# A transformer block pair on one core: token operands of the down projection split in order of use, a third buffer for the high parts of its weights, and its sixth and seventh products exchanged

## The chip, the cores and the metric

The kernel runs on one NeuronCore of a Trainium2 chip. The metric is the device time of one execution in microseconds. The kernel before takes 1577.86 us (median of 3 runs, 1577.79 to 1578.15).

## The reference

Two transformer blocks run one after the other over 512 tokens of width 1024: first a mixer with a mixture of experts, then a mixer, a cross attention and a gated feed-forward layer. The change touches only the last matrix product, the down projection of that feed-forward layer (hidden width 2816 = 22 x 128):

```python
h = rms_norm(x, norm_ffn[l])
x = x + (jax.nn.silu(h @ w_gate[l]) * (h @ w_up[l])) @ w_down[l]
```

All matrices are float32. The kernel keeps that precision by cutting each operand into a high part (rounded to the fast matmul type) and a low part (the rest), and adding three matmuls: high x high, low x high, high x low.

## The kernel before

**The products.** With A the hidden activations (A11, A12 for tokens 0 to 255, A21, A22 for tokens 256 to 511, by halves of the hidden width) and B the weights (B11, B12 / B21, B22, by halves of hidden width and of output columns), the 2 x 2 block product is done with seven products instead of eight (Winograd's form of Strassen's method). In the order of the kernel before they are P1 = A11 B11, P2 = A12 B21, then P6, P7, P4 together, then P3, then P5. Each product has 11 *chunks* (128 rows of the hidden width, 512 output columns). A chunk needs 6 matmuls of 128x512: two token tiles, three matmuls each (`product`). P6, P7 and P4 need sums of the four weight blocks. For these, 11 *triples* T0 to T10 are loaded into one slot each (three rows of 256 KB), a fourth row is added onto one of them by an accumulating DMA of 256 KB from POOL (`add_weights`), and DVE then makes two further sums in place (`weight_sums`, two TENSOR_TENSOR of 128x512; their events are called T2 and T4 in the code, which is not a number of a triple). A triple feeds 18 matmuls. P5 needs the sum of two transferred blocks: each of its three slots is loaded by SP and then gets a second block of 1 MB (the last 768 KB) added onto it by a DMA from POOL (`sums_last`). P3 needs a plain block.

**The slots.** SP issues all loads in order; each waits until PE has freed the slot. Slots 1, 2, 0 serve P1 and again P2; the triples take slots 9, 10, 1, 2, 0, 9, 10, 1, 2, 0, 9; then P3 takes 10, 1, 2 and P5 takes 0, 9, 10, the last of these the slot of P3's first four chunks. So the slot of a triple is that of the triple five before it.

**The splitting.** Chunks are split in *units*: u0 to u5 are P1, u6 to u11 P2 (two chunks each, the sixth one chunk), u12 to u22 the triples T0 to T10, u23 to u34 the last two products. ACT rounds a unit into a cell of the buffer CHH (`unit_high`) and DVE subtracts to make the low part in the slot (`unit_low`); PE waits for the low part. The token operands are split in four pieces each (three chunks, the last two): ACT writes the high piece into a buffer HA (`high_of`), DVE the low piece into AO (`low_of`). A triple uses the pieces of S2, S3 and A22 that hold its chunk. P3 uses S4, P5 uses S1.

**What sets the order.** Each of ACT, DVE and POOL is one queue that runs strictly in the order of the code. The loop over `units` in `scalar` and `vector` is written by hand: at each u it says which pieces, sums and additions onto the output rows (`add_on`) stand there. In `vector` the weight sums of a triple stand ahead of the low part of the unit at which they are called:

```python
if 11 <= u < 11 + FK:
    weight_sums(u - 11)
if u >= len(EARLY_UNITS):
    unit_low(*unit)
```

so the low part of triple j (unit 12 + j) stands behind the sums of triple j + 1.

Of the kernel before, what the change touches and what calls it, by code (L numbers as in the profile page):

```python
# [9 lines left out]
F32R = mybir.dt.float32r  # L10
# [3 lines left out]
ALU = mybir.AluOpType  # L14
# [10 lines left out]
FT = 22  # L25
FK = 11
# [31 lines left out]
GAINED = 33, 38, 46, 52  # L58
FFN_TURN = 11, 15, 27, 33
EARLY_UNITS = 8, 10, 12  # L60


class Issued:
# [6 lines left out]
class Counts:  # L70
# [17 lines left out]
    def at(self, event):  # L88
        if event is None or self.known is None:
            return None, 0  # L90
        name, value = self.known[event]
        return self.sem(name), value
# [278 lines left out]
def _build(nc, t, ctx, force_dense):  # L371
# [8 lines left out]
    at, mark, newest = counts.at, counts.mark, counts.newest  # L380
# [3 lines left out]
    def place(name, kb, n, dt=F32):  # L384
        return nc.alloc_sbuf_tensor_at(name, [P, n * KB], dt, offset=base + kb * 1024)

    CHH = place("CHH", 24, 16, F32R)
    R1, R2 = place("R1", 40, 16), place("R2", 56, 16)
    AH, AL = place("AH", 72, 16, F32R), place("AL", 88, 16, F32R)
    YH, YL = place("YH", 104, 8, F32R), place("YL", 112, 8, F32R)  # L390
# [4 lines left out]
    XTF = place("XTF", 88, 16, F32R)  # L395
    ATF = place("ATF", 168, 8, F32R)
    AR, AO = place("AR", 104, 77), place("AO", 104, 77, F32R)
    HA = [place(f"HA{n}", kb, 11, F32R) for n, kb in enumerate((181, 40, 72, 83, 126))]
    CHX = place("CHX", 52, 4, F32R)
    small_at = [194 * 1024]  # L400

    def sb(name, cols, dt=F32):
# [78 lines left out]
    def plan_slot(i, src, nk, n, part):  # L481
        s = Slot()
        s.number, s.nk, s.n, s.part = len(slots), nk, n, part
        s.src, s.rest, s.more = src, None, None
        s.ap, s.low = (x[i][:, 0:nk * n].rearrange("p (k n) -> p k n", k=nk) for x in (slot_mem, slot_low))
        taken[i] += 1
        s.i, s.landed, s.former, held[i] = i, 16 * taken[i], held[i], s
        slots.append(s)
        return s
# [25 lines left out]
    in_turn = itertools.cycle((2, 0, 1))  # L515
# [23 lines left out]
    in_turn = itertools.cycle((1, 2, 0))  # L539
# [18 lines left out]
    D0 = len(CH)  # L558
    units, hi_of = [], {}

    def unit(s, q0, n, at, ready):
        u = len(units)
        of = CHX if at == 8 else CHH
        a = (0 if at == 8 else at) * 512
        chunks = range(len(CH), len(CH) + n)
        for i, c in enumerate(chunks):
            CH.append((s, q0 + i))
            hi_of[c] = of[:, a + i * 512:a + (i + 1) * 512]
        cells = range(at, at + n)
        before = [holds_cell[x] for x in cells if x in holds_cell]  # L570
        holds_cell.update((x, chunks[-1]) for x in cells)
        units.append((chunks, s.ap[:, q0:q0 + n, :], s.low[:, q0:q0 + n, :],
                      of[:, a:a + n * 512].rearrange("p (k n) -> p k n", k=n), before, ready))
# [1 line left out]
    holds_cell = {(D0 - 1 - x) % 8: D0 - 1 - x for x in range(8)}  # L575
    pair_cells = itertools.cycle((0, 2, 4, 6))

    def plan_block(h, n0, add_row=None):
        for k in range(0, FK, 4):
            m = min(4, FK - k)  # L580
            s = plan_slot(next(in_turn), down_rows[:, h, k:k + m, n0:n0 + 512], m, 512, 3)
            if add_row is not None:
                s.more = down_rows[:, h, k:k + m, add_row:add_row + 512]
            for q in range(0, m, 2):
                unit(s, q, min(2, m - q), next(pair_cells), ("added", s.number) if s.more is not None else None)
# [5 lines left out]
    for j in range(FK):  # L591
        s = plan_slot(next(in_turn), down_rows[:, 0, j, :].rearrange("p (b n) -> p b n", b=2), 3, 512, 3)
        s.rest = down_rows[:, 1, j, 0:512]
        s.more = down_rows[:, 1, j, 512:1024]
        taken[s.i] += 1
        s.landed += 16
        triples.append(s)
        unit(s, 0, 3, 3 * (j % 2), ("T4", j))
    pair_cells = itertools.cycle((6, 8, 3, 0))
    plan_block(1, 512)  # L600
    plan_block(0, 0, add_row=512)
    sums_last = [s for s in slots if s.more is not None][FK:]

    def landed(c):
# [223 lines left out]
    def tensor(pe):  # L828
# [661 lines left out]
        for k in range(FK):  # L1490
            c = D0 + 2 * FK + 3 * k
            product("P6", c, S2, k, sums, False, k == FK - 1)
            product("P7", c + 1, S3, k, own7, k == 0, k == FK - 1)
            product("P4", c + 2, A22, k, own4, k == 0, k == FK - 1)
        banks.next["main"] += 2
        own3 = pair("P3")
        for k in range(FK):
            product("P3", D0 + 5 * FK + k, S4, k, own3, k == 0, k == FK - 1)
        for i in range(2):
            pe.wait_ge(*at(("on x", "P6", 2 + i, 0)))  # L1500
        for k in range(FK):
            product("P5", D0 + 6 * FK + k, S1, k, sums, False, k == FK - 1)
        banks.groups["main"] = (0, 1, 2, 3)


    def scalar(act):
# [718 lines left out]
        def high_of(part, n, *events):  # L2225
            for event in events:
                act.wait_ge(*at(event))
            act.copy(piece(part_high[part], n), piece(parts[:, part], n), scale=-1.0 if part == S1 else 1.0).then_inc(
                *mark("act_evac", ("part high", part, n)))

        gates_done = ("full", "fu20", 1)
        for u, unit in enumerate(units):
            if u >= len(EARLY_UNITS):
                unit_high(*unit)
            if 1 <= u <= 2:
                for n in (2 * u - 2, 2 * u - 1):
                    high_of(A12, n, gates_done, ("a", FT - 1))
            if 3 <= u <= 4:
                for n in (2 * u - 6, 2 * u - 5):
                    high_of(S2, n, ("S4", FK - 1))  # L2240
            if 5 <= u <= 6:
                for n in (2 * u - 10, 2 * u - 9):
                    high_of(S3, n)
            if 10 <= u <= 11:
                for n in (2 * u - 20, 2 * u - 19):
                    high_of(A22, n, ("", "done", D0 + FK - 1))
            if 15 <= u <= 18:
                high_of(S4, u - 15, ("", "done", D0 + 2 * FK - 1))
            if 19 <= u <= 22:
                high_of(S1, u - 19, ("", "done", D0 + 2 * FK - 1))  # L2250


    def vector(dve):
# [914 lines left out]
                dve.tt(xs, *((xs, b, ALU.subtract) if n and name != "P3" else (b, xs, ALU.add))).then_inc(*mark("dve_evac", *events))  # L3168

        for u, unit in enumerate(units):  # L3170
            if 11 <= u < 11 + FK:
                weight_sums(u - 11)
            if u >= len(EARLY_UNITS):
                unit_low(*unit)
            if u == 1:
                first_low(FK - 3)
            if u == 2:
                first_low(FK - 2)
                first_low(FK - 1)
            if 3 <= u <= 4:  # L3180
                for n in (2 * u - 6, 2 * u - 5):
                    low_of(A12, n)
            if 5 <= u <= 6:
                for n in (2 * u - 10, 2 * u - 9):
                    low_of(S2, n)
            if 7 <= u <= 8:
                for n in (2 * u - 14, 2 * u - 13):
                    low_of(S3, n)
            if u == 9:
                add_on("P1", 0, 0)  # L3190
            if 10 <= u <= 11:
                for n in (2 * u - 20, 2 * u - 19):
                    low_of(A22, n)
            if u == 14:
                add_on("P2", 0, 0, left=True, done=True)
            if 15 <= u <= 18:
                low_of(S4, u - 15)
            if 19 <= u <= 22:
                low_of(S1, u - 19)
            if u == 25:  # L3200
                add_on("P6", 1, 0, bank="P1")
            if u == 27:
                add_on("P7", 1, 0)
                add_on("P4", 1, 0, done=True)
            if u == 28:
                add_on("P7", 1, 1)
            if u == 31:
                add_on("P3", 0, 1)
        add_on("P5", 1, 1, bank="P1", done=True)
        add_on("P5", 0, 1, bank="P1", done=True)  # L3210


    def gpsimd(pool):
# [224 lines left out]
        for i in range(NT):  # L3438
            rstd(r4[:, i:i + 1], ss4[:, i:i + 1], 1, 1024.0, ("n4", "sq", i), ("n4", "rs", i))

        for f in range(FT):
            k = f % FK
            pool.wait_ge(*at(("a", f)))
            if f < FK:
                pool.tt(parts[:, S3, k, :], parts[:, A11, k, :], parts[:, A21, k, :], ALU.subtract).then_inc(*mark("pool_down", ("S3", k)))
            else:
                pool.tt(parts[:, S1, k, :], parts[:, A21, k, :], parts[:, A22, k, :], ALU.subtract).then_inc(*mark("pool_down", ("S1", k)))
                pool.wait_ge(*at(("S1", k)))
                pool.tt(parts[:, S2, k, :], parts[:, S1, k, :], parts[:, A11, k, :], ALU.subtract).then_inc(*mark("pool_down", ("S2", k)))
                pool.wait_ge(*at(("S2", k)))  # L3450
                pool.tt(parts[:, S4, k, :], parts[:, A12, k, :], parts[:, S2, k, :], ALU.add).then_inc(*mark("pool_down", ("S4", k)))

        def add_weights(s, to):
            pool.wait_ge(sem(f"w_land{s.i}"), s.landed)
# [173 lines left out]
```

## Time and profile before

| | us |
|---|---|
| median of the runs | 1577.86 |
| the profiled execution | 1577.85 |
| its span | 1576.0 |
| PE busy (97% of the span) | 1530.5 |
| DVE busy | 1061.6 |
| ACT busy | 854.3 |
| first matmul of the down projection | 1449.14 |

Read it so: PE is busy nearly all the time, with a granted clock of 0.995 over the span, so a change shows only where PE stands still or runs at a lower clock. The profiled execution lies on the median, with 1.85 us around its span. In the profile a matmul of 128x512 has a duration of 0.39 us, but they are pipelined: what one costs is the distance between two starts.

### The profile page before, as it was taken

What the parts mean: (1) busy time and instruction counts of PE and PEld (TensorE: products, weight loads), DVE (VectorE), ACT (ScalarE), POOL (GpSimd) and SP (SyncE); (2) the same over time, 40 slices, a digit from 0 to 9 for tenths busy, and PEclk for the clock granted to TensorE, in tenths of its full rate; (3) what the DMA queues carried; (4) which work ended last, traced back from release to release, by engine and by line L of the source; (5) the groups of instructions that cost most, each with busy time, mean ns of one, the idle gap of its engine ahead of it and who ended that gap; (6) DMA issues with size and microseconds to landing.
All of it is one profiled execution on the core that took longest, in us unless ns stands there. A gap on an engine that the chain in (4) does not pass through costs nothing.

```text
span 1576.0 us, 20052 instructions
## 1 busy us (share of the span) xinstructions
PE 1530.5 (97%) x7806; PEld 1238.3 (79%) x7806; DVE 1061.6 (67%) x1717; ACT 854.3 (54%) x1463; POOL 262.7 (17%) x336
## 2 busy tenths in 40 slices
PE   9999999999999999999999999999999999999888
PEld 7877677787887888888877766888778888888766
DVE  4267967866478998999787786675765332345974
ACT  5278776554456888888863434335534332323542
POOL 1000014522234000000172111101201000123110
PEclk9999999999999999999999999999999999999999
DMA  6122121114547999999942111122221332323787
GB/s 236 61 80 81 54 80 55 54 55 159 204 161 233 373 422 420 422 421 421 325 145 101 54 54 54 34 101 66 82 67 55 108 94 94 107 68 125 222 214 193
DMA packets 84849, 250.30 MB, mean 159 GB/s; under 512 B 7536, under 2 KB 10000, under 8 KB 72464
## 3 DMA queue, kind: packets, MB, share of 16 engines
q1 hardware_dynamic: 71456, 216.27, 38.2%
q0 software_dynamic: 6672, 17.85, 4.2%
q10 hardware_dynamic: 6624, 14.88, 2.5%
q8 instruction: 62, 1.02, 0.3%
q14 instruction: 35, 0.29, 0.1%
HBM read 236.39 MB, written 12.60 MB: 158 GB/s over the span
## 4 chain that ended last, share of the span: by engine, by line
PE 76%; DVE 13%; DMA 4%; ACT 3%; issue 1%; POOL 1%; SPq 0%; DVEq 0%; POOLq 0%; ACTq 0%
PE bank L112 70%; PE bank L121 4%; DMA slot<-in_w_down 3%; DVE low L143 2%; PE bank L115 2%; DVE REST L133 1%; DVE REST L143 1%; DVE low L133 1%; DVE REST L146 1%; ACT REST L124 1%; DVE AO L133 1%; ACT REST L127 1%; DVE AL L133 1%; ACT CHH L127 1%; DVE REST L155 1%
## 5 line engine op out<-in xcount | busy, mean ns | idle before, releaser
L133 DVE TENSOR_TENSOR low<-slot,CHH 128x1024 fp32r<-128x1024 f32 (+2 forms) x288 | 312.6, 1126 | 70.4 <-ACT CHH L127 69.5
L127 ACT ACTIVATE CHH<-slot 128x1024 fp32r<-128x1024 f32 (+2 forms) x288 | 269.7, 972 | 115.7 <-PE bank L112 39.9
L143 DVE SCALAR_TENSOR_TENSOR low<-slot,smalls,CHH 128x512 fp32r<-128x512 f32 (+1 forms) x232 | 178.4, 798 | 205.4 <-ACT CHH L127 205.1
L127 ACT ACTIVATE CHH<-slot,smalls 128x512 fp32r<-128x512 f32 (+1 forms) x232 | 156.1, 702 | 172.4 <-PE bank L112 84.6
L112 PE MATMUL bank<-AH,CHH 128*128 128x512 f32 (+1 forms) x640 | 248.5, 388 | 0.2 <-DVE AL L133 0.2
L112 PE MATMUL bank<-AL,CHH 128*128 128x512 f32 (+1 forms) x640 | 242.8, 379 | 0.0
L112 PE MATMUL bank<-AH,low 128*128 128x512 f32 (+1 forms) x640 | 242.5, 379 | 0.0
L112 PE MATMUL bank<-CHH,AH 128*128 128x512 f32 x512 | 215.7, 421 | 3.8 <-DVE low L143 2.8
L112 PE MATMUL bank<-low,AH 128*128 128x512 f32 x512 | 200.9, 392 | 0.0
L112 PE MATMUL bank<-CHH,AL 128*128 128x512 f32 x512 | 200.4, 391 | 0.0
L112 PE MATMUL bank<-CHH,XTF 128*128 128x512 f32 x512 | 161.1, 396 | 1.8 <-DVE REST L130 1.0
L112 PEld LDWEIGHTS bank<-AH,CHH 128*128 128x128 f32 x640 | 120.4, 188 | 23.4 <-issue 1.2
L112 PEld LDWEIGHTS bank<-AL,CHH 128*128 128x128 f32 x640 | 120.4, 188 | 23.0
L112 PEld LDWEIGHTS bank<-AH,low 128*128 128x128 f32 x640 | 120.6, 188 | 20.5
L124 ACT ACTIVATE REST<-REST 128x512 f32<-128x512 f32 (+4 forms) x193 | 97.9, 518 | 46.4 <-POOL REST L133 19.1
L112 PEld LDWEIGHTS bank<-CHH,AH 128*128 128x128 f32 x512 | 97.2, 190 | 29.3 <-issue 6.9
L112 PEld LDWEIGHTS bank<-low,AH 128*128 128x128 f32 x512 | 96.3, 188 | 21.4
L112 PEld LDWEIGHTS bank<-CHH,XTF 128*128 128x128 f32 x512 | 93.5, 188 | 24.0 <-DVE low L133 4.9
L112 PEld LDWEIGHTS bank<-CHH,AL 128*128 128x128 f32 x512 | 97.0, 189 | 15.0
L127 ACT ACTIVATE REST<-bank 128x512 f32<-128x512 f32 (+6 forms) x166 | 62.5, 400 | 70.3 <-PE bank L121 40.7
L112 PE MATMUL bank<-low,XTF 128*128 128x512 f32 x256 | 100.0, 391 | 0.0
L112 PE MATMUL bank<-REST 128*128 128x128 f32 (+8 forms) x688 | 90.0, 306 | 4.9 <-ACT REST L124 2.7
(202 smaller groups left out, 2465.9 us busy)
## 6 DMA issues: line engine op xcount, KB each, us to landing
slot<-in_w_in SPq DMA_DIRECT2D x35, 1024.0 KB, 5.2
slot<-in_w_exp_gate SPq DMA_DIRECT2D x32, 1024.0 KB, 13.3
slot<-in_w_exp_up SPq DMA_DIRECT2D x32, 1024.0 KB, 13.2
slot<-in_w_exp_down SPq DMA_DIRECT2D x32, 1024.0 KB, 13.6
slot<-in_w_gate SPq DMA_DIRECT2D x10, 1024.0 KB, 5.1
slot<-in_w_up SPq DMA_DIRECT2D x10, 1024.0 KB, 5.1
slot<-in_w_out SPq DMA_DIRECT2D x8, 1024.0 KB, 5.9
slot<-in_xkv SPq DMA_DIRECT2D x8, 1024.0 KB, 5.3
```

The lines of the kernel that those rows point to most:

```text
L112: return self.e.matmul(out, l, r, start=start, stop=stop) if self.e else Issued()
L115: return self.e.matmul(out, l, r, start=start, stop=stop, skip_group_check=True) if self.e else Issued()
L121: return self.e.transpose(out, in_, ident) if self.e else Issued()
L124: return self.e.activation(out, in_, f, scale=scale, bias=bias, accum_out=accum) if self.e else Issued()
L127: return self.e.activation(out, in_, ACT.Copy, scale=scale) if self.e else Issued()
L133: return self.e.tensor_tensor(out, a, b, op) if self.e else Issued()
L143: return self.e.scalar_tensor_tensor(out=out, in0=a, scalar=s, in1=b, op0=op0, op1=op1) if self.e else Issued()
L146: return self.e.tensor_tensor_scan(out, a, b, initial, op0, op1) if self.e else Issued()
L155: return self.e.copy_predicated(out, mask, a) if self.e else Issued()
```

## The change

1. The loop over units makes the pieces of the token operands in their order of use. A12 moves from u 1 and 2 to u 3 to 6; S2, S3 and A22 are no longer made four pieces in a row ahead of the triples, but by the tables S2_HIGH, S3_HIGH, A22_HIGH, piece by piece. S1 is now made ahead of S4. The low piece stands one unit later than the high one.
2. The weight sums of a triple stand one unit earlier (`u - 10` for `u - 11`), so the low part of triple j stands behind the sums of triple j + 2.
3. CHH has 9 cells instead of 8 and CHX is gone; the triples turn over three places of three cells instead of two. HA1 moves by 2 KB for that.
4. P5, whose weights are transferred sums, runs before P3. Its slots are those of T6, T7, T8 (10, 1, 2), and P3's are those of T9, T10 (0, 9) and of P5's first block (10).
5. The additions onto the output are moved with them; after the last product two remain instead of four. On POOL the S4 sums of the last two chunks stand behind S1 and S2 of the last chunk.

```diff
+S2_HIGH, S3_HIGH, A22_HIGH = (7, 10, 12, 14), (8, 11, 13, 15), (9, 11, 13, 16)
+S1_HIGH, S4_HIGH = (17, 18, 19, 20), (21, 22, 23, 24)
...
-    CHH = place("CHH", 24, 16, F32R)
+    CHH = place("CHH", 24, 18, F32R)
...
-    HA = [place(f"HA{n}", kb, 11, F32R) for n, kb in enumerate((181, 40, 72, 83, 126))]
-    CHX = place("CHX", 52, 4, F32R)
+    HA = [place(f"HA{n}", kb, 11, F32R) for n, kb in enumerate((181, 42, 72, 83, 126))]
...
-        unit(s, 0, 3, 3 * (j % 2), ("T4", j))
-    pair_cells = itertools.cycle((6, 8, 3, 0))
-    plan_block(1, 512)
-    plan_block(0, 0, add_row=512)
+        unit(s, 0, 3, 3 * (j % 3), ("T4", j))
+    pair_cells = itertools.cycle((6, 0, 2, 4))
+    late = [triples[j].i for j in range(6, FK)]
+    plan_block(0, 0, add_row=512, turns=late[:3])
+    plan_block(1, 512, turns=(*late[3:], late[0]))
...
+        for i in range(2):
+            pe.wait_ge(*at(("on x", "P6", 2 + i, 0)))
+        for k in range(FK):
+            product("P5", D0 + 5 * FK + k, S1, k, sums, False, k == FK - 1)
         banks.next["main"] += 2
         own3 = pair("P3")
         for k in range(FK):
-            product("P3", D0 + 5 * FK + k, S4, k, own3, k == 0, k == FK - 1)
-        for i in range(2):
-            pe.wait_ge(*at(("on x", "P6", 2 + i, 0)))
-        for k in range(FK):
-            product("P5", D0 + 6 * FK + k, S1, k, sums, False, k == FK - 1)
+            product("P3", D0 + 6 * FK + k, S4, k, own3, k == 0, k == FK - 1)
...
         for u, unit in enumerate(units):
-            if 11 <= u < 11 + FK:
-                weight_sums(u - 11)
+            if 10 <= u < 10 + FK:
+                weight_sums(u - 10)
             if u >= len(EARLY_UNITS):
                 unit_low(*unit)
-            if u == 1:
-                first_low(FK - 3)
-            if u == 2:
-                first_low(FK - 2)
-                first_low(FK - 1)
...
+            if 3 <= u <= 5:
+                first_low(FK - 6 + u)
+            if 4 <= u <= 7:
+                low_of(A12, u - 4)
+            for at_units, part in ((S2_HIGH, S2), (S3_HIGH, S3), (A22_HIGH, A22), (S4_HIGH, S4), (S1_HIGH, S1)):
+                if u - 1 in at_units:
+                    low_of(part, at_units.index(u - 1))
...
-        add_on("P5", 1, 1, bank="P1", done=True)
-        add_on("P5", 0, 1, bank="P1", done=True)
+            if u == 32:
+                add_on("P5", 1, 1, bank="P1", done=True)
+            if u == 33:
+                add_on("P5", 0, 1, bank="P1")
+        add_on("P3", 0, 1, done=True)
```

**How the change moves instructions.** In the listings `slot_n` and `low_n` are one slot and the same memory for its low part; AR, HA and AO are the float32, high and low parts of token operands; R is the output rows. The numbers of the kernel before are one higher than those of the changed kernel: slot 0, 1, 2, 9, 10 is slot_81, 82, 83, 90, 91 before and slot_80, 81, 82, 89, 90 in the changed kernel.

DVE at the end of P2, from the low part of u10 to that of u11, in the kernel before:

```order
L133 TENSOR_TENSOR low_92<-slot_81,CHH 128x1024 [waits act_hi]
L133 TENSOR_TENSOR AO<-AR,HA_66 128x768 [waits act_evac] x2
L133 TENSOR_TENSOR slot_90<-slot_90 128x512 [waits w_add9]
L133 TENSOR_TENSOR slot_90<-slot_90 128x512 [waits dve_down]
L133 TENSOR_TENSOR low_92<-slot_81,CHH 128x512 [waits act_hi]
```

and in the changed kernel:

```order
L135 TENSOR_TENSOR slot_89<-slot_89 128x512 [waits w_add9]
L135 TENSOR_TENSOR slot_89<-slot_89 128x512 [waits dve_down]
L135 TENSOR_TENSOR low_91<-slot_80,CHH 128x1024 [waits act_hi]
L135 TENSOR_TENSOR AO<-AR,HA_66 128x768 [waits act_evac]
L135 TENSOR_TENSOR slot_90<-slot_90 128x512 [waits w_add10]
L135 TENSOR_TENSOR slot_90<-slot_90 128x512 [waits dve_down]
L135 TENSOR_TENSOR low_91<-slot_80,CHH 128x512 [waits act_hi]
```

The sums of T0 and T1, which wait for POOL's DMAs, now stand ahead of the low parts of u10 and u11.

DVE among the triples, from the sums of T4 to the low part of T5, in the kernel before:

```order
L133 TENSOR_TENSOR slot_81<-slot_81 128x512 [waits w_add0]
L133 TENSOR_TENSOR slot_81<-slot_81 128x512 [waits dve_down]
L133 TENSOR_TENSOR low_94<-slot_83,CHH 128x1536 [waits act_hi]
L133 TENSOR_TENSOR AO<-AR,HA_68 128x768 [waits act_evac]
L133 TENSOR_TENSOR slot_90<-slot_90 128x512 [waits w_add9]
L133 TENSOR_TENSOR slot_90<-slot_90 128x512 [waits dve_down]
L133 TENSOR_TENSOR low_92<-slot_81,CHH 128x1536 [waits act_hi]
```

and in the changed kernel, from the sums of T4 to the low part of T4:

```order
L135 TENSOR_TENSOR slot_80<-slot_80 128x512 [waits w_add0]
L135 TENSOR_TENSOR slot_80<-slot_80 128x512 [waits dve_down]
L135 TENSOR_TENSOR low_92<-slot_81,CHH 128x1536 [waits act_hi]
L135 TENSOR_TENSOR AO<-AR,HA_69 128x768 [waits act_evac]
L135 TENSOR_TENSOR AO<-AR,HA_66 128x768 [waits act_evac]
L135 TENSOR_TENSOR slot_89<-slot_89 128x512 [waits w_add9]
L135 TENSOR_TENSOR slot_89<-slot_89 128x512 [waits dve_down]
L135 TENSOR_TENSOR low_93<-slot_82,CHH 128x1536 [waits act_hi]
L135 TENSOR_TENSOR AO<-AR,HA_67 128x512 [waits act_evac]
L135 TENSOR_TENSOR slot_90<-slot_90 128x512 [waits w_add10]
L135 TENSOR_TENSOR slot_90<-slot_90 128x512 [waits dve_down]
L135 TENSOR_TENSOR low_91<-slot_80,CHH 128x1536 [waits act_hi]
```

The low part of T4 stands behind the sums of T5 (w_add9) before, and behind those of T6 (w_add10) in the changed kernel.

DVE at the start of the sixth product, from the low part of T10 to P6's two additions onto the output (R), in the kernel before:

```order
L133 TENSOR_TENSOR low_101<-slot_90,CHH 128x1536 [waits act_hi]
L143 SCALAR_TENSOR_TENSOR AO<-AR,HA_70 128x512 [waits act_evac]
L133 TENSOR_TENSOR low_102<-slot_91,CHH 128x1024 [waits act_hi]
L133 TENSOR_TENSOR low_102<-slot_91,CHX 128x1024 [waits act_hi]
L133 TENSOR_TENSOR low_93<-slot_82,CHH 128x1024 [waits act_hi]
L133 TENSOR_TENSOR R_51<-bank,R_51 128x512 [waits pe_dense] x2
```

and in the changed kernel:

```order
L135 TENSOR_TENSOR low_100<-slot_89,CHH 128x1536 [waits act_hi]
L135 TENSOR_TENSOR AO<-AR,HA_68 128x768 [waits act_evac]
L135 TENSOR_TENSOR low_101<-slot_90,CHH 128x1024 [waits act_hi]
L135 TENSOR_TENSOR AO<-AR,HA_68 128x768 [waits act_evac]
L135 TENSOR_TENSOR low_101<-slot_90,CHH 128x1024 [waits act_hi]
L135 TENSOR_TENSOR AO<-AR,HA_68 128x768 [waits act_evac]
L135 TENSOR_TENSOR R_51<-bank,R_51 128x512 [waits pe_dense] x2
```

Between the first low part of the sixth product and P6's additions, for which PE waits before P5, there now stand a second low part and two pieces of S4; and that first low part now rests on a slot that has an accumulating DMA.

## Rows read from the trace of the kernel before

**Rows 1.** PE in order of time: start us, duration us, operation, [idle before, releaser].
```profile
1449.14 0.39 PE L115 MATMUL bank<-CHH,HA 128*128 128x512 f32 x1
...
1458.61 0.47 PE L115 MATMUL bank<-CHH,HA 128*128 128x512 f32 x1 [1.15 <-DVE low L133]
...
1466.43 0.47 PE L115 MATMUL bank<-CHH,HA 128*128 128x512 f32 x1 [0.58 <-DVE low L133]
...
1484.98 0.54 PE L115 MATMUL bank<-CHH,HA 128*128 128x512 f32 x1 [2.89 <-DVE low L133]
...
1504.11 0.50 PE L115 MATMUL bank<-CHH,HA 128*128 128x512 f32 x1 [0.92 <-DVE low L133]
...
1508.65 0.50 PE L115 MATMUL bank<-CHH,HA 128*128 128x512 f32 x1 [0.16 <-DVE low L133]
...
1513.27 0.50 PE L115 MATMUL bank<-CHH,HA 128*128 128x512 f32 x1 [0.24 <-DVE low L133]
...
1524.28 0.50 PE L115 MATMUL bank<-CHH,HA 128*128 128x512 f32 x1 [1.89 <-DVE low L133]
...
1529.67 0.50 PE L115 MATMUL bank<-CHH,HA 128*128 128x512 f32 x1 [1.01 <-DVE low L133]
...
1544.77 0.39 PE L115 MATMUL bank<-CHH,HA 128*128 128x512 f32 x1
...
1547.04 0.39 PE L115 MATMUL bank<-CHH,AO 128*128 128x512 f32 x1
...
1561.38 0.50 PE L115 MATMUL bank<-CHH,HA 128*128 128x512 f32 x1 [2.84 <-DVE low L133]
```

**Rows 2.** Stretches: from:to length, busy us of each engine (instructions), PEclk, DMA.
```profile
1485.00:1488.70 3.70, 3.70 (x9) 2.90 (x10) 3.22 (x4) 0.00 (x0) 0.85 (x1) 0.54 0.69 152
...
1558.00:1561.40 3.40, 0.56 (x4) 0.13 (x2) 1.30 (x2) 2.00 (x2) 0.00 (x0) 1.00 1.13 220
```

**Rows 3.** The chain of waits that ended last: start us, us, what.
```profile
1495.06 0.33 SPq L167
...
1495.43 4.12 DMA slot<-in_w_down
1499.84 5.65 DMA slot<-in_w_down
...
1505.51 0.70 DVE slot L133
...
1506.93 1.68 DVE low L133
...
1520.26 6.25 DMA slot<-in_w_down
...
1543.49 15.50 DMA slot<-in_w_down
```

**Rows 4.** POOL in order of time: the accumulating DMAs of T0, T3, T4 and P5's first.
```profile
1472.81 1.00 POOL L118 DMA_DIRECT2D slot<-in_w_down  x1 [15.43 <-DMA slot<-in_w_down]
...
1483.92 0.84 POOL L118 DMA_DIRECT2D slot<-in_w_down  x1 [6.32 <-DMA slot<-in_w_down]
1487.23 0.85 POOL L118 DMA_DIRECT2D slot<-in_w_down  x1 [2.46 <-DMA slot<-in_w_down]
...
1539.37 1.30 POOL L118 DMA_DIRECT2D slot<-in_w_down  x1 [18.25 <-DMA slot<-in_w_down]
```

**Rows 5.** ACT at P5's first unit, in order of time.
```profile
1549.37 2.01 ACT L127 ACTIVATE CHH<-slot 128x1024 fp32r<-128x1024 f32 x2 [5.12 <-DMA slot<-in_w_down]
```

**Rows 6.** DVE in order of time.
```profile
1456.36 0.43 DVE L133 TENSOR_TENSOR AO<-AR,HA 128x256 fp32r<-128x256 f32 x1 [2.15 <-POOL AR L133]
...
1458.39 1.81 DVE L133 TENSOR_TENSOR AO<-AR,HA 128x768 fp32r<-128x768 f32 x2
...
1488.28 1.42 DVE L133 TENSOR_TENSOR slot<-slot 128x512 f32<-128x512 f32 x2 [0.45 <-DMA slot<-in_w_down]
...
1570.59 2.56 DVE L133 TENSOR_TENSOR R<-R,bank 128x512 f32<-128x512 f32 x4 [3.97 <-PE bank L115]
```

**Rows 7.** DMA issues of 1500 to 1520 us: KB each, median us to landing.
```profile
slot<-in_w_down SPq DMA_DIRECT2D x1, 1024.0 KB, 7.5
```

More of the change, by code:

```diff
@@ L562, in unit @@
         u = len(units)
-        of = CHX if at == 8 else CHH
-        a = (0 if at == 8 else at) * 512
+        of, a = CHH, at * 512
         chunks = range(len(CH), len(CH) + n)
@@ L576, in _build, with plan_block @@
     pair_cells = itertools.cycle((0, 2, 4, 6))
-    def plan_block(h, n0, add_row=None):
+    def plan_block(h, n0, add_row=None, turns=None):
         for k in range(0, FK, 4):
             m = min(4, FK - k)
-            s = plan_slot(next(in_turn), down_rows[:, h, k:k + m, n0:n0 + 512], m, 512, 3)
+            s = plan_slot(turns[k // 4] if turns else next(in_turn), down_rows[:, h, k:k + m, n0:n0 + 512], m, 512, 3)
             if add_row is not None:
@@ L2234, in scalar @@
                 unit_high(*unit)
[L2235 to L2250, printed above, removed]
+            if 3 <= u <= 6:
+                high_of(A12, u - 3, gates_done, ("a", FT - 1))
+            for at_units, part, events in ((S2_HIGH, S2, (("S4", FK - 1),)), (S3_HIGH, S3, (gates_done,)),
+                                           (A22_HIGH, A22, (("", "done", D0 + FK - 1),)), (S4_HIGH, S4, (("", "done", D0 + 2 * FK - 1),)),
+                                           (S1_HIGH, S1, (("", "done", D0 + 2 * FK - 1),))):
+                if u in at_units:
+                    high_of(part, at_units.index(u), *events)
     def vector(dve):
@@ L3170, in vector @@
         for u, unit in enumerate(units):
-            if 11 <= u < 11 + FK:
-                weight_sums(u - 11)
+            if 10 <= u < 10 + FK:
+                weight_sums(u - 10)
             if u >= len(EARLY_UNITS):
                 unit_low(*unit)
-            if u == 1:
-                first_low(FK - 3)
-            if u == 2:
-                first_low(FK - 2)
-                first_low(FK - 1)
[L3180 to L3188, printed above, removed]
+            if 3 <= u <= 5:
[5 more added lines that the diff above has]
+                    low_of(part, at_units.index(u - 1))
             if u == 9:
                 add_on("P1", 0, 0)
[L3191 to L3194, printed above, removed]
+            if u == 16:
                 add_on("P2", 0, 0, left=True, done=True)
[L3196 to L3200, printed above, removed]
+            if u == 24:
                 add_on("P6", 1, 0, bank="P1")
@@ L3206, in vector @@
                 add_on("P7", 1, 1)
-            if u == 31:
-                add_on("P3", 0, 1)
-        add_on("P5", 1, 1, bank="P1", done=True)
-        add_on("P5", 0, 1, bank="P1", done=True)
+            if u == 32:
[3 more added lines that the diff above has]
+        add_on("P3", 0, 1, done=True)
     def gpsimd(pool):
@@ L3439, in gpsimd, with fourth_sum @@
             rstd(r4[:, i:i + 1], ss4[:, i:i + 1], 1, 1024.0, ("n4", "sq", i), ("n4", "rs", i))
+        def fourth_sum(k):
+            pool.wait_ge(*at(("S2", k)))
+            pool.tt(parts[:, S4, k, :], parts[:, A12, k, :], parts[:, S2, k, :], ALU.add).then_inc(*mark("pool_down", ("S4", k)))
         for f in range(FT):
@@ L3449, in gpsimd @@
                 pool.tt(parts[:, S2, k, :], parts[:, S1, k, :], parts[:, A11, k, :], ALU.subtract).then_inc(*mark("pool_down", ("S2", k)))
-                pool.wait_ge(*at(("S2", k)))
-                pool.tt(parts[:, S4, k, :], parts[:, A12, k, :], parts[:, S2, k, :], ALU.add).then_inc(*mark("pool_down", ("S4", k)))
+                if f < FT - 2:
+                    fourth_sum(k)
+        fourth_sum(FK - 2)
+        fourth_sum(FK - 1)
         def add_weights(s, to):
```

## The prediction

> **What bounds the kernel now.** I read the page first (PE busy 97%, so only PE's gaps count), then the stretches from 1300 us on, then PE in order of time in the down projection, then the chain of waits there, and at last POOL, ACT and DVE for what each gap waited on. Starts of matmuls lie 2.27 us apart over ten, 0.227 us each (1544.77 to 1547.04) [rows 1]. The projection has 77 chunks of 6 matmuls, 462 x 0.227 = 104.7 us. It starts at 1449.14 and the last half product is done at 1570.57, just before DVE starts its closing additions [rows 1, 6]; with the 3 matmuls of the other half (0.68) that is 122.1 us. So 17.4 us are lost, in gaps that all end on a DVE low part: 1.15 in P1, 0.58 at P2, 2.89 ahead of T0, 0.92, 0.16, 0.24, 1.89, 1.01 among the triples and 2.84 inside P5 [rows 1], some 0.3 more for each, since idle counts from a matmul's end and not from its start, and 1.7 for nine matmuls at half clock after the gap ahead of T0 (granted clock 0.54 over 3.70 us, where nine take 2.04) [rows 2].
>
> The gaps among the triples have one cause. The chain of waits shows it whole: T1 frees its slot, SP issues the next load of that slot (0.33 and some 0.1), it lands after 4.12, POOL's accumulating DMA follows at 1499.84 and lands after 5.65, DVE makes two sums (2 x 0.70) and then the low part of the triple *before* (1.68), and PE starts [rows 3]. I call this a trip. T1 ended at about 1494.9 (T0 at 1484.98, and 4.08 for 18 matmuls with the restart and the 1.7 of half clock gives 1490.8, plus 4.1), T5 started at 1508.65 [rows 1]: a trip of 13.7 from the end of T(j-4) to the start of Tj. For T4 it is 13.3, for T6 14.3, for T8 (end of T4 at 1508.3) 16.0, for T9 16.6, the last with an accumulating DMA of 6.25 [rows 1, 3]. Between the two ends PE has three triples, 12.2 us, so each trip costs a little. That T0 to T3 ran without a gap is because their slots were loaded early.
>
> **The change part by part.**
>
> *Weight sums one unit earlier.* This is the term that decides. The low part of Tj now stands behind the sums of T(j+2), whose slot is that of T(j-3). The trip is the same, but between its two ends PE has only two triples, 8.2 us. So start(j) = end(j-3) + trip for j = 3 to 8 (T9 and T10 have no sums ahead of them that are not made). The third place for high parts does not help: the releaser in every one of these gaps is DVE's low part, not ACT.
>
> *P1 and P2.* The 1.15 in P1 came from DVE waiting 2.15 for POOL's S2 ahead of the low part of u3 [rows 6]; that wait now stands behind it. DVE also has eight pieces (0.87 each, two of 768 columns take 1.81 with their overlap [rows 6]) less ahead of T0. I take both gaps as gone: P2 starts at 1449.14 + 66 x 0.227 = 1464.1 instead of 1466.43, 2.3 earlier. But the low part of u10, chunk 8 of P2, now stands behind the sums of T0. T0's accumulating DMA was issued at 1472.81 [rows 4]; its load was issued behind one that waited for the end of P1, so I put it 2.3 earlier, 1470.5. It lands after 4.4 (T3's, from 1483.92 until DVE starts on it at 1488.28 [rows 4, 6]) to 5.65 [rows 3]; I take 5.1: 1475.6. Two sums 1.35 and a low part of 1.15 (two thirds of the 1.68 of a triple's): 1478.1, while PE wants it at 1464.1 + 8 x 1.36 = 1475.0. So P2 loses 3.1 and ends at 1482.2 instead of 1481.8 (1466.43 + 15.0 and 0.3 of restarts). DVE then has from 1478.1 on a piece (0.87), T1's sums (1.35), the low part of u11 (0.6), a piece, T2's sums and T0's low part (1.68): T0 starts at 1484.8, where it starts now (1484.98). What the early part gains is given back at once. The wait is again 2.6 and I let the half clock follow as now.
>
> *The triples.* T0 ends at 1490.7, T1 (DVE ready at 1489.4) at 1494.9. T4's accumulating DMA, now issued 5.4 after the end of P2 [rows 4], comes at 1487.6 and lands at 1493.0, then 1.35 and 1.68: T2 runs from 1496.2 to 1500.4. With a trip of 13.5, 13.7, 14, 14, 14, 14.5 for T3 to T8 (from the 13.3 to 16.0 of now, near the lower end since fewer transfers now meet):
> T3 1504.2 to 1508.4; T4 1508.6 to 1512.8; T5 1514.4 to 1518.6; T6 1522.4 to 1526.6; T7 1526.8 to 1531.0; T8 1533.1 to 1537.3; T10 ends at 1545.5.
> Now T6 ends at 1513.27 + 4.2 = 1517.5 and T10 at 1529.67 + 8.3 = 1537.9 [rows 1]. So T6 is 9.1 late and T10 7.6.
>
> *P5 in sixth place.* Its first slot is T6's. From 1526.6: 0.45 for SP, a load of 1 MB between 4.12 (768 KB) and 7.5 [rows 3, 7], I take 5.5, 0.28 to POOL's issue, and an accumulating DMA of 1 MB. There are two rows for that: 10.0 (issued 1539.37 [rows 4], ACT starts on it at 1549.37 [rows 5]) and 15.5 [rows 3]. The first is its likeness, being first in its queue: landed at 1542.8. Then ACT's high part 1.0 (two in 2.01 [rows 5]), DVE's low part 1.2, a piece 0.87, the low part of u24 1.15, a piece 0.87 and P6's two additions 1.2, for which PE waits: 6.4. P5 starts at 1549.2, 3.7 after T10. Its second slot (T7's, free at 1531.0; added 5.7 later and 15.5 long) is landed at 1552.2 and usable at 1554.5, wanted at 1549.2 + 5.4 = 1554.6; its third (T8's) has 1560 as its due and about 1553 to 1558. Both just fit, so the 2.84 inside P5 is gone. P3's plain loads start at 1541.8 and later and are wanted from 1564 on: hidden. P5 and P3 then take 132 x 0.227 = 29.9, less 0.68 for the half and 0.1 for the restart: 1578.6 where it is now 1570.57, +8.0.
>
> *The end.* Four closing additions of 0.64 [rows 6] become two: -1.3. The rest from there to the end of the span stays. S4's sums late on POOL, HA1's place and the ninth cell cost nothing: S4 is wanted after tens of us, and places have no price that the trace shows.
>
> **Sum:** +8.0 - 1.3 = +6.7 on the profiled execution of 1577.85, which is the median of the runs: 1584.5 us.
>
> A rule of the Trainium skill speaks against so late a landing. The page DMA: Bandwidth & Descriptors, in its section on the anatomy of one DMA on the GpSimd path, fits one transfer as about 2.0 us plus its bytes over 436 KB per us, 2.6 for 256 KB and 4.4 for 1 MB. This trace has 5.65 and 10.0 to 15.5 for transfers that also add [rows 3 to 5], so here the measured rows decide. An estimate from that page: trips of 10.3 and 4.4 for P5's addition would end near 1572, a little under rival 3, whose chance covers it.
>
> **The rivals.**
> 1. *Slower still (beyond 1589).* Trips stay near 15 to 16 since P5's 1 MB loads and additions meet the triples' own, and P5's first addition takes 15.5 as the second does now [rows 3]. Trips of 14.9 give T6's end at 1490.7 + 2 x 14.9 + 8.4 = 1528.9, P5's start at 1557.1, +15.9 - 1.3: 1592. For it: T8 and T9 now [rows 1]. Against it: triples half again as far apart. A gap of 3.7 ahead of P5 may also bring back the half clock, +1.7; of the two gaps of nearly 3 us now, one did and one, where the clock stayed 1.00 [rows 2], did not.
> 2. *No change.* The trip falls to 12.4 (loads of 4.12 and 4.4, the shortest here), P5's first addition stays 10.0, and the clock does not fall ahead of T0. T6 ends at 1489.0 + 24.8 + 8.4 = 1522.2, with a load of 5.0 P5 starts at 1544.3: +3.1 - 1.3, 1579.7. It needs the shortest transfer of each kind every time.
> 3. *Faster.* One mechanism: with the triples apart, transfers meet no others, and a trip takes 11, P5's load 4.5 and its addition 8, less than any row of its size. T6 ends at 1519.4, P5 starts at 1539.0, the end is -2.2 - 1.3: 1574.4. It decides from where two trips and P5's addition together fall under 33.6, at which the time is that of now. Against it: already from 1495 to 1508, with little else moving, the trip is 13.7.
> 4. *The change does not do what it says.* P5's weights in time, but the third place for high parts idle. That is inside my forecast.
>
> **How the numbers follow.** The forecast has 0.46 (its own range 1581 to 1589), rival 1 0.18, rival 2 0.22, rival 3 0.14. About 0.2%, 3.2 us, can be told from no change. Slower is the forecast and rival 1, 0.64; same 0.22; faster 0.14. For 8 in 10 the range reaches down through rival 2 to 1577 and up to rival 1's 1592.
>
> **What would show it.** Triples at starts some 6 us apart from T3 on, each gap ended by a DVE low part behind sums that waited for a DMA; a gap in P2 at chunk 8; T0's start near 1485; a gap of 3 to 4 ahead of P5 and none inside it; two closing additions. If the triples follow each other within 4.6 us, the trip or the order on DVE is not what I say, and I am wrong.

## The result and the profile after

| | before | changed kernel |
|---|---|---|
| median of the runs, us | 1577.82 (6 runs, 1576.37 to 1584.09) | 1594.2 (6 runs, 1591.56 to 1597.31) |
| profiled execution, us | 1577.85 | 1591.56 |
| its span, us | 1576.0 | 1589.7 |
| first start of the down projection's matmuls | 1449.14 | 1450.48 |
| first to last start | 121.7 | 135.5 |

The ratio is 1.0101, 95% interval 1.0081 to 1.0121: slower, as forecast, but by 16.4 us in the medians against a forecast of 6.7, and 2 us beyond the upper end of the range. The profiled execution is the shortest of the six of the changed kernel; its span is 13.7 us longer: 13.8 in the projection, 1.3 ahead of it, where the change touches nothing (that start lies between 1446.8 and 1451.5 in the kernels below), and 1.4 less at the end.

PE in order of time, only the starts behind a gap; they answer to [rows 1]:

```profile
1480.12 0.50 PE L117 MATMUL bank<-CHH,HA 128*128 128x512 f32 x1 [3.63 <-DVE low L135]
...
1486.88 0.47 PE L117 MATMUL bank<-CHH,HA 128*128 128x512 f32 x1 [0.79 <-DVE low L135]
...
1491.52 0.50 PE L117 MATMUL bank<-CHH,HA 128*128 128x512 f32 x1 [0.30 <-DVE low L135]
...
1500.40 0.80 PE L117 MATMUL bank<-CHH,HA 128*128 128x512 f32 x1 [4.49 <-DVE low L135]
...
1520.08 0.80 PE L117 MATMUL bank<-CHH,HA 128*128 128x512 f32 x1 [4.99 <-DVE low L135]
...
1540.74 0.80 PE L117 MATMUL bank<-CHH,HA 128*128 128x512 f32 x1 [5.60 <-DVE low L135]
...
1556.14 0.47 PE L117 MATMUL bank<-CHH,HA 128*128 128x512 f32 x1 [0.44 <-DVE R L135]
```

The kernel before had nine gaps of up to 2.89 us and one inside P5. Now there are four large ones, at chunk 8 of P2 and ahead of T2, T5 and T8, each again ended by a DVE low part, and two small ones ahead of T0 and T1. The last line is P5's start. P1 has no gap, and neither have P5 (behind its start) and P3.

The same four places as stretches (clock is the number behind the five engines), answering to [rows 2]:

```profile
1480.00:1485.00 5.00, 4.88 (x14) 3.87 (x15) 4.93 (x9) 1.36 (x3) 0.73 (x1) 0.66 0.53 126
1500.40:1506.90 6.50, 6.50 (x19) 5.19 (x20) 5.66 (x7) 0.31 (x1) 0.85 (x1) 0.65 0.40 81
...
1520.00:1527.00 7.00, 6.92 (x19) 5.49 (x20) 5.50 (x8) 0.61 (x1) 0.85 (x1) 0.61 0.36 56
...
1540.70:1547.00 6.30, 6.26 (x17) 4.96 (x18) 5.67 (x5) 0.57 (x1) 1.27 (x1) 0.58 1.12 203
```

Behind every one of the four gaps the granted clock is 0.58 to 0.66 of full: a good part of the stretch at the lower of the two levels, 1.2 GHz. The 18 matmuls behind each gap take 6.0 to 6.9 us instead of 4.1. In the order of time some 40 matmuls start 0.43 us behind the one before, not 0.23; in the kernel before there were 9.

The chain of waits through T5's gap, answering to [rows 3]:

```profile
1500.40 6.55 PE bank L117 x18
1506.94 0.02 issue
1506.96 0.33 SPq L169
...
1507.33 3.85 DMA slot<-in_w_down
1511.18 0.28 issue
1511.46 5.46 DMA slot<-in_w_down
...
1518.36 1.68 DVE low L135
...
1520.08 6.91 PE bank L117 x18
```

T2 ends at 1506.94, its slot's next load and addition land at 1516.9, and T5 starts at 1520.08, a trip of 13.1. DVE in order of time says who stands behind what:

```profile
1516.94 1.42 DVE L135 TENSOR_TENSOR slot<-slot 128x512 f32<-128x512 f32 x2 [5.48 <-DMA slot<-in_w_down]
1518.28 1.75 DVE L135 TENSOR_TENSOR low<-slot,CHH 128x1536 fp32r<-128x1536 f32 x1
...
1585.70 1.37 DVE L135 TENSOR_TENSOR R<-bank,R 128x512 f32<-128x512 f32 x2 [7.38 <-PE bank L117]
```

DVE stands 5.48 us at T7's sums, while T5's low part, whose data had landed long before, waits behind them. The last line is the closing additions, two instead of the four of [rows 6].

### The profile page after: what moved, and what is told of

Read it like the earlier page. It is cut to its first block, busy times and chain, and to the rows that moved or that the text cites. A ratio compares the mean times of both kernels' runs of the same rounds, so it can differ in the third digit from the quotient of the medians.

```text
span 1589.7 us, 20054 instructions
## 1 busy us (share of the span) xinstructions
PE 1537.7 (97%) x7806; PEld 1244.8 (78%) x7806; DVE 1062.3 (67%) x1717; ACT 854.9 (54%) x1463; POOL 263.5 (17%) x336
## 4 chain that ended last, share of the span: by engine, by line
PE 79%; DVE 12%; DMA 4%; ACT 3%; issue 1%; POOL 1%; SPq 0%; DVEq 0%; POOLq 0%; ACTq 0%
PE bank L114 71%; PE bank L117 5%; PE bank L123 4%; DMA slot<-in_w_down 3%; DVE low L145 2%; DVE REST L135 1%; DVE REST L145 1%; DVE REST L148 1%; ACT REST L126 1%; DVE AL L135 1%; DVE low L135 1%; DVE REST L157 1%; ACT REST L129 1%; DVE REST L154 1%; ACT CHH L129 1%
```

## The experiments

All ratios are to the kernel before in its own runs on the same chip, where its median was 1579.7 to 1580.8 us.

### Sums back at u - 11

```diff
-            if 10 <= u < 10 + FK:
-                weight_sums(u - 10)
+            if 11 <= u < 11 + FK:
+                weight_sums(u - 11)
```

> The changed kernel with the weight sums of a triple one unit later, where the kernel before has them (unit u makes the sums of triple u - 11); all else stays changed. Theory 1 (the place of the sums on DVE is what costs): the low part of Tj again stands behind the sums of T(j+1), so triples start about 4.6 us apart instead of the 6.6 measured from T2 to T8, no stretch at half clock among them, no stall at chunk 8 of P2; P5 starts at most 3 us after T10 ends. 1572 to 1577 us, some 20 less than the changed kernel's 1594.2. Rival A (the sixth place of P5, whose slots need 1 MB additions among the triples' loads, or the pieces in order of use, cost the time): stays at 1588 or above.

Measured: 1579.17 us (12 runs), ratio 0.9990 (0.9977 to 1.0003). One edit takes back all of the loss; rival A is out. The time is 2 us above the stated interval, but the kernel before also took 3 us more in these runs, so by the ratio it lies inside. What missed is P5's start, which was to come at most 3 us after T10:

```profile
1508.51 0.50 PE L117 MATMUL bank<-CHH,HA 128*128 128x512 f32 x1 [1.79 <-DVE low L135]
...
1527.89 0.47 PE L117 MATMUL bank<-CHH,HA 128*128 128x512 f32 x1 [0.66 <-DVE low L135]
1544.13 0.76 PE L117 MATMUL bank<-CHH,HA 128*128 128x512 f32 x1 [7.83 <-DVE R L135]
```

T5 to T9 start within 19.4 us, 4.8 us apart, with no half clock among them (ahead of T0 there still is some: 0.55 behind a gap of 2.30). But P5 in sixth place now waits 7.83. Its chain:

```profile
1517.97 6.89 DMA slot<-in_w_down
...
1525.15 12.47 DMA slot<-in_w_down
...
1537.64 1.06 ACT CHH L129
...
1542.83 1.21 DVE R L135 x2
```

From T6's end (1517.96) to P5's start 26.2 us; the prediction's terms for it made 22.6.

### Sums at u - 12

> The changed kernel with the sums two units later (unit u makes the sums of triple u - 12), so the low part of Tj stands behind its own sums alone. Theory 1: PE then has four triples, 16.3 us, between the end of T(j-5) and the start of Tj, against a trip of 13.7 plus some 1.5 for the high part that now follows the sums in series, 15.2: no gaps among the triples, 4.1 us each; 1570 to 1575 us. Rival A: 1588 or above. Rival B (the serial high part eats the extra triple): as with u - 11 or 1 to 3 us worse than it.

The edit is the same line with 12. Measured: 1583.20 us (12 runs), ratio 1.0017 (1.0004 to 1.0030). Theory 1's number is missed; rival B holds, at 4 us worse than u - 11 even somewhat more than it said. One triple of the chain of waits:

```profile
1507.13 0.70 DVE slot L135
...
1507.86 1.50 ACT CHH L129
...
1509.38 1.76 DVE low L135
1511.14 0.60 DVE AO L135
1511.74 0.61 DVE slot L135
```

No DMA stands in it: sums, ACT's high part, low part, piece, sums again, in series, with DVE idle while ACT works. The triples start 5.2 to 6.4 us apart, where one takes 4.1. So one unit of lead is worth having (it hides ACT's 1.50), two are too many (they let DVE wait for a DMA).

### The kernel before with sums at u - 10

> The kernel before with this one edit of the change: unit u makes the sums of triple u - 10 instead of u - 11. Theory 1: gaps of 4 to 6 us at every third triple, each followed by some 12 matmuls at half clock, and a stall late in P2: 1586 to 1594 us against 1577.8. Rival A (product order or pieces): no change, 1576 to 1579.

Measured: 1595.28 us (6 runs), ratio 1.0089 (1.0070 to 1.0108), within the interval of the whole change (1.0081 to 1.0121). The same signature:

```profile
1510.41 0.79 PE L115 MATMUL bank<-CHH,HA 128*128 128x512 f32 x1 [4.55 <-DVE low L133]
...
1531.10 0.80 PE L115 MATMUL bank<-CHH,HA 128*128 128x512 f32 x1 [5.67 <-DVE low L133]
```

P2's stall is there too (3.18 us). The time is 1.3 us above the stated interval; the ratio is inside what that interval gives. With the first experiment this settles the place: the edit is sufficient and necessary for the loss.

### Unused matmuls in the gaps

```diff
+            if k in (5, 8):
+                for i in range(2):
+                    pe.wait_ge(*at(("free", ("P2", i))))
+                for n in range(12):
+                    pe.matmul_on(own2[n % 2], HA[1][:, 0:P], HA[1][:, 0:512], True, True)
```

> The changed kernel with 12 more matmuls (2.7 us, their results used nowhere) ahead of T5 and of T8, on the two banks that P2 has left, so that PE stands still for some 2.3 us instead of 5.0 and 5.6 there. Nothing of the DVE order changes, so T5 and T8 start when they did. Theory 2 (the idle time ahead of T5 and T8 drops the granted clock, which then costs about 2.6 us at each): granted clock 1.00 through T5 and T8, 18 matmuls in 4.2 us instead of 6.9 and 6.7, and the time 4 to 6 us shorter than the changed kernel's 1594.2. Rival C (the slow matmuls after a gap come from something else, operands or memory, not from the idle time): the same 6.9 and 6.7 us, and no change of the time.

Measured: 1590.94 us (6 runs), ratio 1.0062 (1.0043 to 1.0080) against the changed kernel's 1.0101 (1.0081 to 1.0121): 3.3 us less in the medians, 6 by the ratios, and the intervals do not overlap. PE in order of time and the stretches behind the two starts:

```profile
1513.78 2.88 PE L117 MATMUL bank<-HA 128*128 128x512 f32 x12
...
1518.89 0.50 PE L117 MATMUL bank<-CHH,HA 128*128 128x512 f32 x1 [2.23 <-DVE low L135]
...
1537.22 0.50 PE L117 MATMUL bank<-CHH,HA 128*128 128x512 f32 x1 [2.71 <-DVE low L135]
```

```profile
1518.80:1525.00 6.20, 6.08 (x25) 4.71 (x26) 5.38 (x8) 2.21 (x3) 0.85 (x1) 1.00 0.50 82
...
1537.20:1543.40 6.20, 6.18 (x20) 4.95 (x21) 5.64 (x5) 0.55 (x1) 1.27 (x1) 0.72 1.05 193
```

Behind 2.23 us of idle the clock stayed at 1.00 and 25 matmuls ran in 6.2 us; behind 2.71 it fell for a part of the stretch (0.72), where 1.00 was expected. More work for PE, and yet less time: the idle time costs the clock on top of itself. Rival C is out. I had expected T8 to start when it did; it started 3.5 us earlier (1537.22 for 1540.74), because its trip begins at the end of T5, which came 3.8 earlier, 1.2 by T5's start and the rest by the full clock. (This profiled execution also has a gap of 3.50 inside P5, with the clock at 0.51 behind it, that the changed kernel's has not. It is 2 us longer than the changed kernel's, so the gain rests on the six runs and not on this pair of profiles.)

### P3 sixth again, with the rest of the change

The first experiment's kernel with the two last products in the old order and on the old slots, S4's pieces at units 17 to 20 and S1's at 21 to 24, and four closing additions.

```diff
-    plan_block(0, 0, add_row=512, turns=late[:3])
-    plan_block(1, 512, turns=(*late[3:], late[0]))
+    plan_block(1, 512, turns=late[:3])
+    plan_block(0, 0, add_row=512, turns=(*late[3:], late[0]))
```

> The first experiment's kernel (changed kernel, sums at u - 11) with P3 sixth and P5 last again, on the slots of the kernel before (P3 on those of T6, T7, T8, P5 on those of T9, T10 and P3's first block), S4's pieces ahead of S1's and four closing additions again. Theory 3 (in sixth place P5 waits for its 1 MB addition, 8.0 us in the first experiment, where last it waits 3.0 in its middle; the two closing additions saved give 1.3 back): P3 starts right behind T10, and the whole is 3 to 4 us shorter than the first experiment's 1579.2, 1575 to 1577, ratio to before 0.9965 to 0.998. Rival D (the exchange is worth what it was made for): 1 to 4 us longer than the first experiment.

Measured: 1577.50 us (12 runs), ratio 0.9986 (0.9974 to 0.9997). That is just outside the stated 1575 to 1577 and 0.9965 to 0.998. PE has no gap ahead of P3, and 2.64 inside P5. The profile has the mechanism; but the times do not tell this kernel from the first experiment (0.9990), so neither theory 3's gain of 3 to 4 us nor the lower end of rival D is settled by them. This kernel is also the change without its parts 2 and 4 (it has the pieces in order of use, the third place for high parts and POOL's new order): a small gain over the kernel before, 2 us.

### P5's blocks on earlier slots

```diff
-    plan_block(1, 512, turns=late[:3])
-    plan_block(0, 0, add_row=512, turns=(*late[3:], late[0]))
+    plan_block(1, 512, turns=(late[0], late[3], late[4]))
+    plan_block(0, 0, add_row=512, turns=(late[1], late[2], late[0]))
...
+        loads[-6:] = [loads[n - 6] for n in (0, 3, 4, 1, 2, 5)]
```

> As the run before it, but P5's first two blocks take the slots of T7 and T8, and P3's last two those of T9 and T10; SP issues them in the order in which the slots come free. So P5's additions of 1 MB start some 8 us earlier while P3's plain loads are still in time (needed 5.4 and 10.9 us after T10, landed 4 and 8 after it). Theory 3: no gap inside P3 or P5, 3 us less than with the old slots, 1572 to 1575, ratio 0.9945 to 0.9965. Rival E (the additions and the plain loads slow each other, so that the wait only moves into P3): the same as with the old slots.

Measured: 1579.63 us (12 runs), ratio 0.9999 (0.9988 to 1.0011). Theory 3's gain is missed; rival E holds. The same deal in the kernel before:

> The kernel before with only the slots of the last two products dealt out as in the second run of this job (P5's first two blocks on the slots of T7 and T8). Theory 3: the gap of 3.0 inside P5 goes, nothing else changes: 1577 to 1578.5 where before is 1580.8 on this chip, ratio 0.997 to 0.9985. Rival E: no change or a gap in P3 in its place.

Measured: 1582.61 us (12 runs), ratio 1.0015 (1.0005 to 1.0026): again no gain, even a small loss. The gap inside P5 is gone in both, and a larger one stands in P3 (5.07 and 6.39 us). The chain of waits of the second:

```profile
1533.62 13.48 DMA slot<-in_w_down
...
1547.13 1.06 ACT CHH L127
...
1548.21 1.23 DVE low L133
...
1549.49 26.91 PE bank L115 x105
```

A plain load of 1 MB, 5.0 us at the median of the eight in the down projection of the kernel before, takes 13.48 while two additions of 1 MB run. The DMA queues over 1530 to 1550 us:

```profile
q0 software_dynamic: 1056, 2.10, 57.4%
q1 hardware_dynamic: 1585, 3.15, 46.0%
```

The first line is POOL's queue, which here carries the additions, the second SP's with the loads and some output rows. POOL's holds over half of the 16 engines' time for 2.1 MB, SP's 46% for 3.15 MB: together all of it. So the additions are dear: 27% of the engines' time over these 20 us per MB (5.5 us of all 16 engines) against 15% (2.9 us). From 1530 to 1575 us in the changed kernel the same two numbers come out: 38.8% of 45 us for 3.15 MB, and 45.5% for 7.09 MB.

### P6's additions ahead of P5's first low part

```diff
+            if u == 23:
+                add_on("P6", 1, 0, bank="P1")
             if u >= len(EARLY_UNITS):
                 unit_low(*unit)
```

(in the first experiment's kernel; the same call at u == 24 is gone, and S1_HIGH, S4_HIGH = (16, 17, 18, 19), (18, 19, 20, 21))

> The first experiment's kernel (P5 sixth) with P6's two additions onto the output ahead of P5's first low part on DVE, and the pieces of S1 and S4 one to three units earlier, so that nothing but the first high and low part stands between the landing of P5's first addition and its first matmul. Theory 3 with my term of 6.4 us for that stretch: P5 starts 2.4 instead of 6.5 us after the landing, 4 us earlier; P5's second block, landed at 1545.9 and usable at 1548.2 there, then makes a gap of up to 2.8 in P5. Net 1 to 4 us less than the first experiment: 1575 to 1578. Rival F (PE could have started without these, they only fill DVE's wait): no change.

Measured: 1578.18 us (12 runs), ratio 0.9991 (0.9979 to 1.0002), the first experiment's 0.9990 again. P5's wait is 3.93 instead of 7.83, and P5 starts 2.5 us behind the landing (the addition issued at 1523.74 took 14.5), as theory 3 has it, but three gaps of 0.70, 0.26 and 0.67 follow inside P5 and P3, where the first experiment has none:

```profile
1540.77 0.47 PE L117 MATMUL bank<-CHH,HA 128*128 128x512 f32 x1 [3.93 <-DVE low L135]
1548.78 0.50 PE L117 MATMUL bank<-CHH,HA 128*128 128x512 f32 x1 [0.70 <-DVE low L135]
```

The time does not tell it from the first experiment; theory 3's gain of 1 to 4 us did not show.

### The exchange undone in the changed kernel

The kernel with P3 sixth, and the sums at u - 10.

> The changed kernel (sums at u - 10 kept) with only the exchange of the last two products undone: P3 sixth on the slots of T6, T7, T8, P5 last on those of T9, T10 and P3's first block, four closing additions. My account: the slow triples leave P5's first addition time to land, so in the changed kernel the sixth place costs nothing (0.6 us wait) and saves the 3 us gap inside P5 and two closing additions (1.3): without it 3 to 5 us more than the changed kernel, 1597 to 1600 against a before of about 1580, ratio 1.011 to 1.014. Rival: P5 sixth costs in the changed kernel too, as with fast triples (8.0 us): 3 us or more less, ratio 1.006 to 1.008.

Measured: 1596.78 us (4 runs), ratio 1.0105 (1.0089 to 1.0120), against 1.0101 with the exchange. Just under the interval that I gave, and not told apart from the changed kernel by the times; the rival's 1.006 to 1.008 is out. The profiles lean to my account: first to last start 138.0 us against 135.5, with 2.53 of idle inside P5, but they are one execution each.

### Unused matmuls in the P3-sixth kernel

```diff
+            if k == 0:
+                pe.wait_ge(*at(("part", S2, 0)))
+                for n in range(6):
+                    pe.matmul_on((own7 + own4)[n % 4], HA[1][:, 0:P], HA[1][:, 0:512], True, True)
+            if k == 8:
...
+                for n in range(4):
+                    pe.matmul_on(own2[n % 2], HA[1][:, 0:P], HA[1][:, 0:512], True, True)
```

> The P3-sixth kernel with sums at u - 11 (measured 0.9986 of before) with 6 unused matmuls (1.4 us) ahead of T0 and 4 (0.9 us) ahead of T8, where PE stood still for 2.3 and 2.2 us and then ran 7 matmuls each at half clock. Theory 2 (the idle stretch drops the clock): granted clock 1.00 behind both, 1.5 us saved at each, ratio 0.996 to 0.9975. Rival C (not the idle time): no change or the fillers' own length more, 0.9986 to 1.000.

Measured: 1577.04 us (11 runs), ratio 0.9978 (0.9967 to 0.9989), the best of all kernels here. PE in order of time:

```profile
1479.05 1.52 PE L117 MATMUL bank<-HA 128*128 128x512 f32 x6
1481.42 0.50 PE L117 MATMUL bank<-CHH,HA 128*128 128x512 f32 x1 [0.85 <-DVE low L135]
...
1517.96 1.07 PE L117 MATMUL bank<-HA 128*128 128x512 f32 x4
1524.31 0.50 PE L117 MATMUL bank<-CHH,HA 128*128 128x512 f32 x1 [1.20 <-DVE low L135]
```

Ahead of T0 (1481.42) 0.85 us of idle is left where the kernel without them had 2.31, and the clock stays 1.00 where it was 0.61. The second place was a slip of mine: the gap of 2.19 with a clock of 0.59 behind it stands ahead of T9 there, not of T8; T8 starts 0.9 later for the four matmuls, and T9's gap is 1.20 with a clock of 1.00. The interval of the kernel without them (0.9974 to 0.9997) overlaps this one, so the gain over it leans only on the profile; against the kernel before it is clear, 0.2%. The ratio lies just above the interval that I gave (0.996 to 0.9975). Inside P5 this execution has a gap of 2.77 us with the clock at 0.64 behind it, where the kernel without the unused matmuls had 2.64 and 1.00; so a part of the gain was lost again there.

## Why the prediction was right in its sign and wrong in its size

- **Weight sums one unit earlier: right, and the term that decides.** Shown by adding and by removing it. The trips were as taken: T2's end to T5's start 13.1, T5's end (1527.0) to T8's start 13.7, against 14 and 14.5 predicted. The shape was not: T3's and T4's low parts were ready by 1505.3 and 1509.7, before PE wanted them, so the gaps bunch, one of 4.5 to 5.6 us at every third triple (T2, T5, T8), where the prediction's own starts have 3.8 ahead of T3 and T6, 1.3 to 2.1 ahead of T2, T5 and T8 and 0.2 at T4 and T7. In sum the two are near: 15.1 measured, 13.0 predicted.
- **The half clock: this step failed.** "The wait is again 2.6 and I let the half clock follow as now", and rival 1 had one more stretch of 1.7. That is one stretch at half clock, ahead of T0, and none for gaps of 3.1 in P2 and twice 3.8 among the triples, though a gap of 2.89 had dropped the clock in the rows. Measured, the gap ahead of T0 is 0.79 and the clock behind it stayed 1.00, while it fell behind each of the four long gaps (0.58 to 0.66). 40 instead of 9 matmuls at 0.43 us make 31 x 0.2 = 6.2 us. The projection grew by 13.8, so the gaps themselves by 7.6, where the prediction had 8.0 for all. The term missing from the sum is the clock, +6.2. It stands on the path, since each next trip begins only when T2 or T5 has ended, and the experiments with unused matmuls confirm it as a cost of idle time.
- **P1 and P2: right but for T0.** P1's gap went, and the low part of u10 stalled behind T0's sums: 3.1 predicted, 3.63 idle measured, with the clock again on top. I had the next trip start from P2's end at 1482.2; it ended at 1486.1, of which 1.3 is the later start of the whole, 0.7 the gap and 1.8 the clock. The 2.6 of wait ahead of T0 became 0.79, since P2 ended 3.9 late and T0 started only 2.1 late.
- **P5 in sixth place: the terms right here, the wait not.** POOL's row for P5's first addition in the changed kernel:

```profile
1536.66 1.30 POOL L120 DMA_DIRECT2D slot<-in_w_down  x1 [4.04 <-DMA slot<-in_w_down]
```

The load ahead of it took 5.3 and the addition itself 9.0, against my 5.5 and 10.0. It landed at 1545.7, and the wait ahead of P5 was 0.44 instead of 3.7, since T7 to T10 came so late that PE was not yet there. That takes 3.3 us off the sum and hides a part of what the clock added. With the fast triples of the first experiment both were longer: 6.89 for the load and 12.47 for the addition, and 7.83 of wait. The 6.4 behind the landing were 6.5 there. The gap inside P5 went as said.
- **The end: right.** 1.3 predicted, 1.4 measured.
- **The rivals.** The faster one, with trips of 11, did not come. Rival 1's time (1592) is the nearest, but by luck: it had longer trips and a slow addition, and neither came. The third place for high parts of rival 4 was never tried alone. The fit of the Trainium skill's page DMA: Bandwidth & Descriptors (section on the anatomy of one DMA on the GpSimd path) gives 2.6 us for 256 KB and 4.4 for 1 MB. The trace does not agree for transfers that add: 3.94 to 5.81 us for the triples' additions on the changed kernel's chain, 9.0 for P5's first there and 12.47 in the first experiment.
- **Open:** the six runs' median lies 2.6 us above the profiled execution. How often the clock falls may vary from run to run, but the other five have no profile. The ninth cell alone was not tried, nor the exchange with the kernel before's order of pieces.

## What to carry to other kernels

On an engine that runs in order, ask of every operation moved forward which DMA it waits for and what already complete work it then holds up; compare the trip of a reused buffer with the work left between its two ends, for each lead (here one unit was best, zero serialised DVE with ACT, two made DVE wait for DMA). Gaps that are bound by a common trip can bunch together, as they did here, and a long gap costs twice, once as idle time and once as half clock behind it: give the clock a term of its own for each gap of some 2 us and more, and try a few unused matmuls in it. A transfer that adds took nearly twice as much of the DMA engines' time per MB as a plain one here, so starting it earlier slowed the loads beside it.

## What the runs showed of the hardware beyond that

- Over the down projections of all these kernels, the clock fell behind every idle stretch of 3.50 us and more (17 of them). Below that the length alone did not decide it: it fell behind 1.95 (0.68 in the changed kernel with the sums at u - 12), 2.19, 2.30, 2.31, 2.53, 2.71, 2.77, 2.89 and 2.90 us, and stayed at 1.00 behind 2.06 (in that same kernel), 2.23, 2.64, 2.74, 2.84 and 3.18 us. The last is from the kernel before with sums at u - 10:

```profile
1483.20 0.50 PE L115 MATMUL bank<-CHH,HA 128*128 128x512 f32 x1 [3.18 <-DVE low L133]
```

- A plain load of 1 MB took 5.0 us at the median, 12.17 and 13.48 beside two accumulating ones (the two kernels with P5's blocks on earlier slots).
